# Layer 0's input projection: six of its tiles in three pairs by seven products, and the modulation blocks dealt in halves of one chunk

## What is computed

```python
mx = split((silu(c)    @ w_mod[l] + b_mod[l]), 6)      # 6 vectors of 1024 for x
mc = split((silu(c_ctx) @ w_mod[l] + b_mod[l]), 6)     # the same for ctx
zx = modulate(rms_norm(x,   norm1_g[l]), mx[0], mx[1]) @ w_in[l]
zc = modulate(rms_norm(ctx, norm1_g[l]), mc[0], mc[1]) @ w_in[l]
f, cq, ckv, kr, g = split(z, (256, 512, 640, 672))     # g: 512 columns, a and gate
# f:  FNet mixing;  cq, ckv, kr: latent attention (rms_norm of cq and ckv, rope of kr)
# g:  u = a * sigmoid(gate); u = depthwise_conv31(u) + b; silu(layer_norm(u)) @ w_pw2
```

## Time and profile before

| | us |
|---|---|
| median of 3 runs | 1803.23 (1799.43 to 1803.93) |
| the profiled execution, device time | 1798.18 |
| its span in the trace | 1796.4 |
| TensorE busy in the span | 1720.8 |
| granted TensorE clock, mean of the span | 0.992 |

### The profile page before, as it was taken

One profiled execution on the slowest core, in us unless ns is written; L12 is line 12 of the kernel. 1 busy time (PEld: TensorE's weight loads), 2 busy tenths in 40 slices (PEclk: granted clock), 3 DMA queues, 4 the chain that ended last, 5 costly groups with the idle time before them and its releaser, 6 DMA issues.

```text
span 1796.4 us, 27176 instructions
## 1 busy us (share of the span) xinstructions
PE 1720.8 (96%) x10930; PEld 1379.4 (77%) x10930; DVE 980.5 (55%) x1881; ACT 415.9 (23%) x806; POOL 315.4 (18%) x349
## 2 busy tenths in 40 slices
PE   7999999899999999899899999999999999999997
PEld 5434454488888888665799998877888788799996
DVE  1238652365676434577378754377731432288883
ACT  1312553222111210226322101322421101211110
POOL 0100262122001221005134201068000000001110
PEclk9999999999999999999999999999999999999999
DMA  7784472232333222330345545434222443344452
GB/s 281 298 322 192 142 272 105 71 117 94 116 119 117 88 77 94 140 135 30 117 163 167 165 166 187 141 118 141 95 72 72 146 160 118 109 152 162 164 181 101
DMA packets 38710, 256.32 MB, mean 143 GB/s; under 512 B 4128, under 2 KB 7328, under 8 KB 9024
## 3 DMA queue, kind: packets, MB, share of 16 engines
q1 hardware_dynamic: 36240, 240.87, 38.3%
q0 software_dynamic: 1776, 9.57, 1.4%
q10 hardware_dynamic: 576, 4.19, 0.6%
HBM read 247.28 MB, written 7.34 MB: 142 GB/s over the span
## 4 chain that ended last, share of the span: by engine, by line
PE 84%; DVE 8%; ACT 2%; DMA 2%; issue 1%; POOL 1%; SPq 0%; ACTq 0%; DVEq 0%; POOLq 0%
PE ps L668 83%; DMA ring<-weights 1%; PE ps L901 1%; POOL aux L1912 1%; DMA xT<-x_t 1%; DVE arena L2121 1%; DVE aux L2150 1%; DVE arena L2151 1%; DVE arena L2152 1%; ACT hT L1527 0%; POOL aux L1895 0%; DVE ring L2195 0%; DVE aux L2055 0%; DVE aux L2057 0%; DVE aux L2060 0%
## 5 line engine op out<-in xcount | busy, mean ns | idle before, releaser
L668 PE MATMUL ps<-hT,ring 128*128 128x256 f32 (+3 forms) x3024 | 670.7, 383 | 16.8 <-ACT hT L1527 4.7
L668 PEld LDWEIGHTS ps<-hT,ring 128*128 128x128 f32 (+1 forms) x3024 | 520.2, 191 | 155.0 <-issue 97.3
L668 PE MATMUL ps<-arena,ring 128*128 128x256 f32 (+3 forms) x1884 | 355.4, 343 | 4.7 <-DVE arena L2152 3.4
L668 PEld LDWEIGHTS ps<-arena,ring 128*128 128x128 f32 (+1 forms) x1884 | 298.5, 191 | 50.9 <-issue 13.0
L668 PE MATMUL ps<-arena,sums 128*128 128x128 f32 (+1 forms) x966 | 161.6, 317 | 1.3 <-DVE aux L2221 1.3
L668 PEld LDWEIGHTS ps<-arena,sums 128*128 128x128 f32 x966 | 141.7, 191 | 12.3 <-DVE aux L2221 2.5
L1895 POOL TENSOR_TENSOR aux<-aux 128x256 f32<-128x256 f32 (+1 forms) x46 | 49.3, 1072 | 439.9 <-ACT aux L1462 370.9
L2194 DVE TENSOR_TENSOR sums<-ring 128x512 f32<-128x512 f32 x83 | 57.6, 694 | 66.5 <-PE ps L668 59.3
L668 PE MATMUL ps<-hT,sums 128*128 128x128 f32 (+1 forms) x592 | 89.9, 300 | 0.5 <-DVE aux L2221 0.5
L1912 POOL TENSOR_SCALAR aux<-aux,small 128x512 f32<-128x512 f32 (+1 forms) x48 | 71.0, 1486 | 86.9 <-DVE small L2170 86.3
L1931 POOL TENSOR_TENSOR arena<-arena 128x256 f32<-128x256 f32 (+1 forms) x32 | 26.4, 826 | 333.8 <-ACT arena L1651 333.8
(11 more groups left out here) (368 smaller groups left out, 1934.6 us busy)
## 6 DMA issues: line engine op xcount, KB each, us to landing
ring<-weights SPq DMA_DIRECT2D x224, 1024.0 KB, 4.9
kept_turns<-aux ACTq DMA_DIRECT2D x4, 1024.0 KB, 5.7
arena<-kept_turns POOLq DMA_DIRECT2D x6, 512.0 KB, 6.3
kept_keys_values<-spare POOLq DMA_DIRECT2D x1, 2048.0 KB, 8.2
arena<-kept_keys_values POOLq DMA_DIRECT2D x1, 2048.0 KB, 9.2
tab<-tables SPq DMA_DIRECT2D x1, 1344.0 KB, 13.9
arena<-mem_t SPq DMA_DIRECT2D x2, 512.0 KB, 5.5
xT<-ctx_t SPq DMA_DIRECT2D x1, 1024.0 KB, 9.1
```

The source lines that it names most:

```text
L668: ins = nc.tensor.matmul(o_, lhsT, rhs, start=start, stop=stop, skip_group_check=True)
```

## The change

Layer 0 alone. Tiles 8 and 9, 0 and 1, 4 and 5 become three pairs, each by seven products (`z_quad`) from a chunk of its own. Tiles 6, 7, 2 and 3 stay as they were. The sixteen half blocks of the modulation (one chunk of weights each, 4 matmuls) are dealt over the seven items by the table `Z_FIRST`. The activation forms lie where qT comes later (`z_form`). VectorE makes the forms and the first weight sums at the head of the stage, the second sums after 6 taps, the second combination after 20, the third sums after 24, the third combination behind the normalisation of ckv. ScalarE no longer copies the six tiles; it copies the first product of each pair, and squares or takes the sigmoid from SBUF after the combination. `kr_sum` and `mod_turn` come behind all items. 24 taps are early, 16 in the middle and 22 in the attention. `weight_sums` and `combined` are moved up unchanged but for a branch for the pairs of z. Conditions that counted pairs from 0 now count from the MLP's first.

```diff
-TAPS_EARLY = (46, 34)
-TAPS_MIDDLE = (0, 16)
+TAPS_EARLY = (24, 34)
+TAPS_MIDDLE = (16, 16)
+TAPS_PARTS = (6, 20)
+Z_FIRST = ((6, 2), (7, 3), ((8, 9), 3), (2, 2), ((0, 1), 3), (3, 0), ((4, 5), 3))
+Z_SEVEN = (4, 0, 2)
...
+        if l == 0:
+            part = 2 * MOD_FIRST
+            for item, halves in Z_FIRST:
+                if isinstance(item, tuple):
+                    whole()
+                    p = item[0] // 2
+                    for role in range(4):
+                        for j in range(4):
+                            k, n = j + 4 * (role % 2), item[role // 2]
+                            out.append((("zq", 0, 0, p, 0, role, j), "w_in", 0, z_tile(0, n, k)))
+                else:
+                    for k in range(KD if item != 3 else KD // 4):
+                        out.append((("z", 0, item, k), "w_in", 0, z_tile(0, item, k)))
+                for _ in range(halves):
+                    mod(0, part // 2, 4 * (part % 2), 4 * (part % 2) + 4)
+                    part += 1
...
+                def z_quad(p):
+
+                    n_quad = quad_first[0, 0, "zq", p, 0]
+                    for i, (wf, af) in enumerate(PRODUCTS):
+                        b, o = divmod(i * T, 512)
+                        key = ("zq", 0, 0, p, b)
+                        if o == 0:
+                            open_bank(key)
+                        for j in range(4):
+                            r = z_act(af, j, n_quad == 0)
+                            if wf in ROLES:
+                                lhsT = weight(("zq", 0, 0, p, 0, ROLES[wf], j))
+                            else:
+                                lhsT = sums[:, n_quad % 2, SUMS[wf], j * P:(j + 1) * P]
+                            if i == 2 and j == 0:
+                                pe.wait_ge(S["quad_sums"], n_quad + 1)
+                            mm(bank(key)[:, o:o + T], lhsT, r, o == 0 and j == 0, j == 3,
+                               key if j == 3 and (o + T == 512 or i == 6) else None)
...
+                if l == 0:
+                    part = 2 * MOD_FIRST
+                    for i, (item, halves) in enumerate(Z_FIRST):
+                        if isinstance(item, tuple):
+                            z_quad(item[0] // 2)
+                        else:
+                            z_plain(item, i == 0)
+                        if item == 3:
+                            latent_sums()
+                        for _ in range(halves):
+                            mod_block(0, part // 2, 4 * (part % 2), 4 * (part % 2) + 4)
+                            part += 1
+                    kr_sum(0)
+                    mod_turn(0, 1)
...
+                if l == 0:
+                    dve.wait_ge(S["h_ready"], KD)
+                    b11, b12 = hT[:, 0:4, half_a(0)], hT[:, 0:4, half_b(0)]
+                    b21, b22 = hT[:, 4:8, half_a(0)], hT[:, 4:8, half_b(0)]
+                    did(tt(z_form[0], b12, b11, ALU.subtract), "z_forms")
+                    did(tt(z_form[1], b22, b12, ALU.subtract), "z_forms")
+                    did(tt(z_form[2], b22, z_form[0], ALU.subtract), "z_forms")
+                    did(tt(z_form[3], b21, z_form[2], ALU.subtract), "z_forms")
+                    weight_sums(0)
                 finished(dve, ("z", l, 6))
                 did(v.memset(upad[:, :, :, :], 0.0))
+                if l == 0:
+                    combined(0, "zq", 0, Z_SEVEN[0])
...
-                for tap, k in rest[:TAPS_EARLY[l]]:
+                for n, (tap, k) in enumerate(rest[:TAPS_EARLY[l]]):
+                    if l == 0 and n == TAPS_PARTS[0]:
+                        weight_sums(1)
+                    if l == 0 and n == TAPS_PARTS[1]:
+                        combined(0, "zq", 0, Z_SEVEN[1])
                     conv_tap(tap, k)
+                if l == 0:
+                    weight_sums(2)
```

More of the change, by code:

```diff
@@ L405, in two_blocks @@
         qT = flat[:, o:o + 4096].rearrange("p (h t) -> p h t", h=HEADS)
+        z_form = [flat[:, o + 1024 * i:o + 1024 * (i + 1)].rearrange("p (j t) -> p j t", t=T) for i in range(4)]
         o += 4096
@@ L699, in mod_block @@
                 key = ("modp", l, part)
-                if q == first:
+                if q == first and k0 == 0:
                     open_bank(key, "mod")
@@ L792, in _, with z_act, z_plain @@
                     mod_block(1, MOD_LATE + 2, 0, 4)
[L794 to L798, removed]
+                def z_act(form, j, first):
+                    if form in ("b11", "b21", "b22"):
+                        return hT[:, j + (0 if form == "b11" else 4), half_b(0) if form == "b22" else half_a(0)]
+                    f = ("t1", "t3", "t2", "t4").index(form)
+                    if first and j == 0:
+                        pe.wait_ge(S["z_forms"], f + 1)
+                    return z_form[f][:, j, :]
+                def z_quad(p):
[15 more added lines that the diff above has]
+                               key if j == 3 and (o + T == 512 or i == 6) else None)
+                def z_plain(n, first):
                     key = ("z", l, n)
@@ L801, in _, with ready @@
                     o_ = open_bank(key)
-                    def ready(k, i=i, n=n, l=l):
-                        if i == 0:
+                    def ready(k):
+                        if first:
                             pe.wait_ge(S["h_ready"], KD * l + k + 1)
@@ L2081, in _, with weight_sums @@
             quad_done = [0]
+            def weight_sums(n):
+                c, b = quad_chunk[n], n % 2
+                dve.wait_ge(landed[c % SLOTS], 16 * (c // SLOTS + 1))
+                if n >= 2:
+                    dve.wait_ge(chunks_used, quad_chunk[n - 2] + 1)
+                a11, a12, a21, a22 = (ring[:, c % SLOTS, 4 * i:4 * i + 4, :].rearrange("p a b -> p (a b)") for i in range(4))
+                s2, s3, s4 = (sums[:, b, i, :] for i in range(3))
+                did(tt(s3, a11, a21, ALU.subtract))
+                did(tt(a21, a21, a22, ALU.add))
+                did(tt(s2, a21, a11, ALU.subtract))
+                did(tt(s4, a12, s2, ALU.subtract), "quad_sums", wait=False)
@@ L2184, in _ @@
                     did(v.tensor_tensor(conv[:, k, s], conv[:, k, s], rinv2[:, s], ALU.mult), "conv_scaled")
[L2186 to L2197, removed]
@@ L2278, in _ @@
                         weight_sums(n + 2)
-                    if n == 1:
+                    if l == 0 and n == first + 1:
                         s5_turn_rate()
-                    if n == 4:
+                    if l == 0 and n == first + 4:
                         s5_factors()
```

165 lines of the change are left out of this document (98 added, 67 removed).

## The result

The changed kernel takes 1807.36 us (median of 17 runs, 1805.12 to 1810.18) against 1802.13 us (17 runs, 1797.60 to 1805.79) for the kernel before in the same set. The ratio is 1.0032, with a 95% interval of 1.0024 to 1.0039: 5.2 us slower. The profiled execution took 1806.51 us, its span is 1804.7 us against 1796.4 us before. Among all executions behind this document one, of e8_taps_middle, was slow as a whole (3009.01 us at a mean granted clock of 0.556) and is left out of the comparisons.

A forecast was written before the change was run, and what follows sets the result against it. TensorE was taken to bound the kernel (busy 96% of the span). 2.0 us for the stage, 0.3 for taps and 2.6 for the clock, less 0.3 for a copy, gave +4.6 us: 1807.8 us, range 1800 to 1813.

The forecast's parts named there:

- The mechanism: Layer 0 stage: TensorE waits for weights 2.9, 3.2 and 3.2 us ahead of the first pair, tile 2 and tile 3.
- Rows 6: Trace rows at layer 1's start: three modulation chunks, then a z tile starting 6.03 us after their beginning, 3.25 us idle.
- it is the latency that counts and not the rate: Ring of weights: a chunk takes 4.9 us from issue to landing, against 2.46 us at full rate.
- The saving: TensorE in the stage: a pair by seven products takes 12.09 us, two plain tiles 14.06; three pairs save 5.9 us.
- The stage without the clock: Stage up to the DFTs: 9.3 us of new waits against 6.8 us saved and 0.5 rounding; ends 2.0 us later.
- The clock: TensorE's clock behind the three waits: one or two falls of 3.4 us, costing 1.7 to 3.4 us, 2.6 taken.
- VectorE: VectorE in the stage: weight sums hidden by 0.5 us, squares by 2.8 us, the last chain by 2 us.
- only because of the wait ahead of tile 3: Squares after pair (0, 1)'s combination: the 2.8 us by which they are hidden exists only through that wait.
- The 0.3 us for taps in the attention: Six more taps in attention steps 16 to 21 cost 0.3 us, between bounds of nothing and 4.7 us.
- Transfers in time: Rival: the stage's waits are absent or short as DMA is only 0.73 busy; 6.8 us gained, 1796.4 us; chance 0.1.
- The clock kept: Rival: the three waits come but the clock stays up; +2.3 us, 1805.5 us; chance 0.2.
- Falls behind all three waits: Rival: lowered clock behind every wait, one in the long form; 9.1 us slower, 1812.3 us; chance 0.2.

The follow-up runs named there:

- e8_taps_middle: e2_reorder with 22 taps in the middle in place of 16, and 16 in the attention; 1799.28 us.
- e1_redeal: The changed kernel with halves dealt (3, 2, 2, 2, 2, 2, 3) in place of (2, 3, 3, 2, 3, 0, 3), same item order; 1798.89 us.
- e2_reorder: The changed kernel with halves (3, 2, 2, 2, 2, 2, 3), pair (0, 1) before tile 2, second weight sums before the first combination; 1794.33 us.
- e4_plain_pairs: The changed kernel with each pair's two tiles multiplied plainly from the same chunks, without forms, weight sums or combinations; 1812.87 us.
- e3_fill: The changed kernel with matmuls whose result is overwritten in its three waits: two, three and three of 512 columns; 1802.76 us.
- e7_taps_late: e2_reorder with 6 taps in the middle in place of 16, so all 32 attention steps carry a tap; 1794.73 us.
- e6_one_wait: e2_reorder with one half moved from behind tile 3 to behind pair (8, 9); 1803.47 us.
- e9_one_wait_early: e6_one_wait with the combination of pair (0, 1) after 14 taps in place of 20; 1799.44 us.
- e10_one_wait_fill: e9_one_wait_early with three matmuls of 512 columns, result overwritten, in the wait ahead of pair (0, 1); 1800.24 us.
- e5_same_again: The kernel of e2_reorder unchanged, repeated on another chip as reference; 1793.79 us.

## Why the prediction was right

- *The mechanism.* The three waits came where they were put: 2.57, 3.44 and 3.42 us for 2.9, 3.2 and 3.2 predicted, and none ahead of the other two pairs. Rows 6 carried this. The small difference is that from the run's beginning to the next item it is 6.2 us here, and not 6.03. The remark that "it is the latency that counts and not the rate" holds for the first 2 us, in which no byte moves; behind that the DMA engines are busy at 0.91 to 1.00 and move 381 to 419 GB/s in all three waits, so some 4.2 of the 6.2 us are transfer. e1_redeal and e2_reorder take the waits away by the deal alone, e4_plain_pairs keeps them with other multiplications.
- *The saving.* 5.9 us predicted for three pairs, with 12.09 us from the MLP for one. Here a pair takes 12.3 us, so three save 5.4 to 5.5 against two plain tiles each; e4_plain_pairs puts 4.9 of them down to the seven products. The term was 0.5 us too large.
- *The stage without the clock.* +2.0 us predicted. The changed kernel's stage is 5.7 us longer with 2.9 us of low clock in it, so 2.8; e3_fill gives 2.9. The 0.8 to 0.9 us more are the dearer pairs (0.5), the 0.63 us ahead of the third half behind tile 7, where 0.31 were assumed, and 0.1 us in the three waits.
- *The clock.* I took 2.6 us, one fall or two of 3.4 us. In the profile there was one of 6.8 us behind the first and shortest of the three waits (2.9 us lost), and none behind the other two. Over all executions the estimate is 3.2 us (mean granted clock 0.9884 against 0.9902), and the rest is 2.4. e3_fill is 4.6 us faster than the changed kernel, with the two intervals some 2 to 7 us, which is more than the 2.6 us; by the estimates 4.2 us of it are the clock's. I drew no line between what a fall costs in the stage and later: between the attention's end and the second pair of the MLP the changed kernel's profile loses another 3.3 us (its pair starts at 376.75 us, 9.0 us behind the earlier trace rows, where the step at 274.6 us was 5.7 us behind). 1.6 of them are a fall at 283.5 us that the kernel before does not have. The other 1.7 lie in the MLP's first pair: before, the clock is low there for 6.8 us in one piece, after the change for 3.4 us at 358.6 and, behind a longer wait, for 3.4 us at 368.8. TensorE's timelines of the kernel before and then of the changed kernel:

```profile
360.77 1.99 PE L668 MATMUL ps<-spare,ring 128*128 128x256 f32 x8 [0.76 <-DVE spare L2266]
```
```profile
368.05 3.08 PE L686 MATMUL ps<-spare,ring 128*128 128x256 f32 x8 [2.25 <-DVE spare L2373]
```

Of the twelve profiles, the six with a fall shortly behind the attention have the second form here, and the six without it the first. Whether the change makes either likelier was not shown.
- *The number.* 1807.8 was forecast and 1807.36 measured. That it is so close is partly luck: the three runs of the kernel before had a median of 1803.23, 1.1 us above that of all seventeen, and the step was 5.2 us and not 4.6.
- *VectorE.* The weight sums were hidden and the squares in time, as predicted, and so was the remark that the latter held "only because of the wait ahead of tile 3": e1_redeal has no such wait, and 2.39 us for the squares in its place. The 0.3 us for taps in the attention is not to be seen (e7_taps_late).
- *The rivals.* Transfers in time: refuted by the timeline. The clock kept: true of many places, but not of the sum. Falls behind all three waits: not in this profile. The Trainium skill (TensorE: Matmul & The Clock Gate, HAM oscillation) tells of a kernel that lost its clock behind every wait for a transfer, with waits of about 3 to 5 us. The trace agrees only in part: it held here for the 3.27 us and 3.30 us waits of e6_one_wait and e9_one_wait_early, for two waits of three in e4_plain_pairs (3.29 and 3.40 us, not 3.36), and for one of three in the changed kernel.

## What to carry to other kernels

In a ring, the chunks that follow a chunk must keep TensorE busy at least as long as a freed slot takes to fill: here three chunks of 0.93 us each against 6.2 us, and that, not the mean rate of 248 GB/s, decides. A stage whose DMA engines are busy for only 0.64 of the time can still wait again and again, so saving arithmetic pays only once short and long items are dealt for it; with the same work, dealing two halves behind the first two pairs in place of three turned +5 us into -3 us, and moving one pair and its weight sums forward as well gave -8 us. A late chunk is paid for up to three times, in the wait, in the clock behind it, and in every queue whose head waits for the same chunk, so look for all three before pricing it.

## What the runs showed of the hardware that I had not expected

The same gap lowers the clock in one execution and not in another. TensorE's gap of 2.42 us ahead of 65.8 us was passed at full clock by the kernel before; in e10_one_wait_fill, up to there the same program, the gap was 2.34 us and the clock was low from 66.6 us on. The window of e10_one_wait_fill:

```profile
66.60:70.00 3.40, 3.40 (x14) 0.50 0.00 0
```

A gap of 2.57 us was followed by 6.8 us at the lower level, gaps of 3.44 and 3.42 us by none. Nor does it take 2 us: ahead of the first pair both e5_same_again and e7_taps_late, the same program up to there, wait 1.48 us. The first goes on at full clock, the second at the lower one, so the same eight matmuls take 3.69 and 5.38 us (e5_same_again, then e7_taps_late, whose wait of 0.55 us came shortly before):

```profile
105.24 3.69 PE L686 MATMUL ps<-hT,ring 128*128 128x256 f32 x16 [1.48 <-DMA ring<-weights]
```
```profile
102.41 1.06 PE L686 MATMUL ps<-ring,raw 128*32 128x512 f32 x8 [0.55 <-DMA ring<-weights]
104.96 5.38 PE L686 MATMUL ps<-hT,ring 128*128 128x256 f32 x16 [1.48 <-DMA ring<-weights]
```

The clock goes with most of the spread between executions of one kernel. Over 69 executions of the kernel before, the ten with a mean granted clock of 0.992 took 1798.5 us in the mean and the four with 0.988 took 1804.8. So only medians of many runs could tell these kernels apart; what is left of the spread was not traced.
